# The second half of a macaron block's last feed-forward layer: 16 of its 22 row tiles by Strassen's scheme

## The reference, cut to what matters

```
h = rmsnorm(x, ffn2_pre_norm)
gate, up = split(h @ w_ffn2_in, 2)          # w_ffn2_in: 1024 x 5632
a = silu(gate) * up                         # a: 512 tokens x 2816
y = a @ w_ffn2_out                          # w_ffn2_out: 2816 x 1024
x = x + 0.5 * rmsnorm(y, ffn2_post_norm)
```

## Time and profile before

| | us |
|---|---|
| three runs, lowest, median, highest | 1472.89, 1472.93, 1472.98 |
| the profiled execution, first to last instruction (span) | 1471.1 |
| TensorE matmul busy | 1463.6 |
| VectorE, ScalarE busy | 735.7, 592.3 |
| the layer's second half, first to last matmul | 119.7 |

### The profile page before, as it was taken

One profiled execution on the slowest core, in us unless ns is written; L12 is line 12 of the kernel. 1 busy time (PEld: TensorE's weight loads), 2 busy tenths in 40 slices (PEclk: granted clock), 3 DMA queues, 4 the chain that ended last, 5 costly groups with the idle time before them and its releaser, 6 DMA issues.

```text
span 1471.1 us, 20399 instructions
## 1 busy us (share of the span) xinstructions
PE 1463.6 (99%) x7600; PEld 1226.3 (83%) x7600; DVE 735.7 (50%) x1219; ACT 592.3 (40%) x969; POOL 20.2 (1%) x35
## 2 busy tenths in 40 slices
PE   9999999999999999999999999999999999999998
PEld 7888888888898888888888888888889888888886
DVE  6444444224763455554257776654447544444223
ACT  5233223223543455554254654553345432323222
POOL 0000000000100000000000000000000000000000
PEclk9999999999999999999999999999999999999999
DMA  5322322334232222212322222223331323332332
GB/s 194 99 89 97 100 100 86 100 101 130 76 124 99 78 72 90 73 64 94 99 87 72 72 73 69 71 72 129 105 111 44 101 87 99 100 99 89 98 100 100
DMA packets 39399, 137.70 MB, mean 94 GB/s; under 512 B 4743, under 2 KB 4743, under 8 KB 39344
## 3 DMA queue, kind: packets, MB, share of 16 engines
q1 hardware_dynamic: 37728, 132.14, 27.9%
q0 software_dynamic: 1472, 4.76, 1.2%
q10 hardware_dynamic: 144, 0.04, 0.0%
HBM read 134.00 MB, written 2.13 MB: 93 GB/s over the span
## 4 chain that ended last, share of the span: by engine, by line
PE 99%; DMA 0%; DVE 0%; ACT 0%; issue 0%; DVEq 0%; SPq 0%; ACTq 0%
PE ps L333 28%; PE ps L335 27%; PE ps L334 27%; PE ps L1468 1%; PE ps L1204 1%; PE ps L1205 1%; PE ps L1206 1%; PE ps L1347 1%; PE ps L1346 1%; PE ps L1348 1%; PE ps L1828 1%; PE ps L1448 1%; PE ps L1848 1%; PE ps L1433 1%; PE ps L1815 1%; PE ps L1435 1%
## 5 line engine op out<-in xcount | busy, mean ns | idle before, releaser
L333 PE MATMUL ps<-hh,whi 128*128 128x512 f32 x1232 | 485.9, 394 | 0.0
L291 ACT ACTIVATE whi<-raw 128x1024 fp32r<-128x1024 f32 x232 | 245.7, 1059 | 585.4 <-PE ps L335 530.2
L334 PE MATMUL ps<-hl,whi 128*128 128x512 f32 x1232 | 480.0, 390 | 0.0
L335 PE MATMUL ps<-hh,wlo 128*128 128x512 f32 x1232 | 479.9, 390 | 0.0
L296 DVE TENSOR_TENSOR wlo<-raw,whi 128x1024 fp32r<-128x1024 f32 x232 | 284.1, 1225 | 368.1 <-ACT whi L291 368.0
L333 PEld LDWEIGHTS ps<-hh,whi 128*128 128x128 f32 x1232 | 231.4, 188 | 53.0 <-issue 2.8
L335 PEld LDWEIGHTS ps<-hh,wlo 128*128 128x128 f32 x1232 | 231.4, 188 | 48.9
L334 PEld LDWEIGHTS ps<-hl,whi 128*128 128x128 f32 x1232 | 231.6, 188 | 46.6 <-issue 0.2
L514 DVE TENSOR_TENSOR tmp<-ps,rstd 128x512 f32<-128x512 f32 x44 | 30.4, 690 | 118.8 <-PE ps L335 118.8
L333 PE MATMUL ps<-ah,whi 128*128 128x512 f32 (+1 forms) x192 | 71.6, 373 | 0.4 <-DVE wlo L296 0.4
L334 PE MATMUL ps<-al,whi 128*128 128x512 f32 (+1 forms) x192 | 71.3, 371 | 0.0
(11 more groups left out here) (318 smaller groups left out, 1854.1 us busy)
## 6 DMA issues: line engine op xcount, KB each, us to landing
raw<-in_wstream SPq DMA_DIRECT2D x238, 512.0 KB, 3.4
xt<-in_x_t SPq DMA_DIRECT2D x8, 256.0 KB, 5.3
out<-out_tok SPq DMA_DIRECT2D x8, 256.0 KB, 2.0
bias<-vec_dram POOLq DMA_DIRECT2D x8, 192.0 KB, 3.2
raw<-in_wstream SPq DMA_DIRECT2D x4, 256.0 KB, 4.4
bias<-vec_dram POOLq DMA_DIRECT2D x8, 128.0 KB, 3.4
raw_y<-in_wstream SPq DMA_DIRECT2D x2, 512.0 KB, 4.2
raw_x<-in_wstream SPq DMA_DIRECT2D x2, 512.0 KB, 4.1
```

What stands on the lines that cost most here:

```text
L291: nc.scalar.activation(whi[:, s, :], raw[:, s, :], ACT.Copy).then_inc(head_done, 1)
L333: nc.tensor.matmul(out, w, m, start=start, stop=False)
L334: nc.tensor.matmul(out, w, ml, start=False, stop=False)
L335: return nc.tensor.matmul(out, wl, m, start=False, stop=stop)
```

## The change

The last 16 row tiles of the second half are computed by a scheme of Strassen's kind (Winograd's form: 7 products, 4 sums of each operand, 7 joins). Tokens, columns and row tiles are each cut in two halves, so that both operands have four quarters. The even of the 16 tiles are one half, the odd the other; `kp` numbers the eight pairs, and a chunk `c` is two of them. In place of 8 products of quarters there are 7; each is 2 token tiles x 2 tiles x 3 = 12 matmuls a chunk (`quadrant`), with a block of its own that is one quarter of the weights of that chunk.

- The layer's first half is written out from turn 6 on for ACT and DVE (`pair`). The tile of `a` is kept whole (`a_raw`, in the place of `al`). Per pair, DVE makes four sums of 128 x 256 (`pair_sums`), each waiting for the one before; ACT makes the high parts of both tiles (1024 columns) and of three sums (768), and DVE the low parts (`pair_head`, `pair_low`). Pairs 6 and 7 get theirs in the second half.
- The second half has 34 blocks m for 22: 12 DIRECT ones (three quarters of each chunk, as they are), 16 SUMMED ones (four quarters of each chunk, which are loaded again and on which DVE first makes a sum in place, `w_sum`), and 6 plain ones of 24 matmuls for the first 6 row tiles.
- Split blocks have three buffers for two, and loaded ones a ring of six for two (`out_load`).
- Results of products are copied from PSUM by ACT (`leave`) and joined by DVE with what others hold (the joins).
- The new buffers lie where `x` by token and the gain row were. So POOL stores `x` to memory at turn 5 and loads it and the gain row again when the plain blocks begin.
- Some semaphores elsewhere are merged, with the same order of work.

The core of the diff (left out: the places of buffers, `t_sums`, `raw_slot`, `plain`, the definitions of most joins, which each are one DVE instruction of 128 x 512, and the merged semaphores):

```diff
+N_KP = 8
+N_PLAIN = FT - 2 * N_KP
+N_CHUNK = N_KP // 2
+AHEAD_KP = 6
+LAST = 2 * FIRST["ffn3_out"]
+DIRECT, SUMMED = 3 * N_CHUNK, 4 * N_CHUNK
+PLAIN_0 = DIRECT + SUMMED
+OUT_BLOCKS = PLAIN_0 + N_PLAIN
+RING = 6
...
+        a_raw = place("a_raw", [P, FT, S])
...
+        def pair_sums(dve, m):
+            k1, k2 = N_PLAIN + 2 * m, N_PLAIN + 2 * m + 1
+            raw_t = t_sums(m)[2].rearrange("p (t n) -> p t n", t=3)
+            a = [[a_raw[:, k, cols] for cols in TOKENS] for k in (k1, k2)]
+            if m < 2:
+                dve.wait_ge(sem("x_turned"), KT)
+            elif m < AHEAD_KP:
+                dve.wait_ge(sem("pool_stored"), 16 * (1 + TT))
+            else:
+                dve.wait_ge(block_done, LAST)
+            dve.wait_ge(sem("glu"), BEFORE[3] + k2 + 2)
+            nc.vector.tensor_tensor(raw_t[:, 1, :], a[1][1], a[0][1], ALU.subtract).then_inc(sem("t_sum"), 1)
+            dve.wait_ge(sem("t_sum"), 4 * m + 1)
+            nc.vector.tensor_tensor(a[0][1], a[0][0], a[0][1], ALU.subtract).then_inc(sem("t_sum"), 1)
+            dve.wait_ge(sem("t_sum"), 4 * m + 2)
+            nc.vector.scalar_tensor_tensor(out=raw_t[:, 0, :], in0=a[0][1], scalar=-1.0, in1=a[1][1], op0=ALU.mult,
+                                           op1=ALU.subtract).then_inc(sem("t_sum"), 1)
+            dve.wait_ge(sem("t_sum"), 4 * m + 3)
+            nc.vector.scalar_tensor_tensor(out=raw_t[:, 2, :], in0=raw_t[:, 0, :], scalar=-1.0, in1=a[1][0],
+                                           op0=ALU.mult, op1=ALU.subtract).then_inc(sem("t_sum"), 1)
+        def pair_head(act, m):
+            k1 = N_PLAIN + 2 * m
+            high, _, summed = t_sums(m)
+            flat = "p k n -> p (k n)"
+            act.wait_ge(sem("t_sum"), 4 * m + 2)
+            act.wait_ge(sem("glu"), BEFORE[3] + k1 + 3)
+            nc.scalar.activation(ah[:, k1:k1 + 2, :].rearrange(flat), a_raw[:, k1:k1 + 2, :].rearrange(flat),
+                                 ACT.Copy).then_inc(sem("a_head"), 1)
+            act.wait_ge(sem("t_sum"), 4 * m + 4)
+            nc.scalar.activation(high, summed, ACT.Copy).then_inc(sem("a_head"), 1)
+        def pair_low(dve, m, part):
+            k1 = N_PLAIN + 2 * m
+            flat = "p k n -> p (k n)"
+            dve.wait_ge(sem("t_sum"), 4 * m + 4)
+            dve.wait_ge(sem("a_head"), BEFORE[3] + k1 + part + 1)
+            high, low, whole = t_sums(m) if part else [x[:, k1:k1 + 2, :].rearrange(flat) for x in (ah, al, a_raw)]
+            nc.vector.tensor_tensor(low, whole, high.bitcast(F32), ALU.subtract
+                                    ).then_inc(sem("a_tail"), 1)
...
+            def pair(m):
+                j = N_PLAIN + 2 * m
+                for k in (j, j + 1):
+                    turn(k, False)
+                if m < AHEAD_KP:
+                    pair_head(act, m)
...
+            def glu_whole(j):
+                dve.wait_ge(sem("silu"), BEFORE[n] + j + 2)
+                dve.wait_ge(sem("up"), BEFORE[n] + j + 1)
+                nc.vector.tensor_tensor(a_raw[:, j, :], silu[:], tmp[:, 1, :], ALU.mult
+                                        ).then_inc(sem("glu"), 1)
+            def pair(m):
+                j = N_PLAIN + 2 * m
+                gated(j, 0)
+                tail(dve, first + j, 0)
+                if 0 < m <= AHEAD_KP:
+                    for part in range(2):
+                        pair_low(dve, m - 1, part)
+                up(j, 1)
+                tail(dve, first + j, 1)
+                glu_whole(j)
+                gated(j + 1, 0)
+                tail(dve, first + j + 1, 0)
+                up(j + 1, 1)
+                tail(dve, first + j + 1, 1)
+                glu_whole(j + 1)
+                if m < AHEAD_KP:
+                    pair_sums(dve, m)
...
+        BANK_U, BANK_V, BANK_W, BANK_Z = (4, 5), (6, 7), (2, 3), (0, 1)
+        ROW_BANK = (BANK_U + BANK_V, BANK_W + BANK_Z)
+        FIRST_HALF = (2, 3, 0, 1)
...
+        def split_of(m):
+            s = m % 3
+            return (whi[:, s, :], wlo[:, s, :]) if s < 2 else (whi_2[:], wlo_2[:])
+        def out_source(m):
+            if m < DIRECT:
+                return (m % 3) * N_CHUNK + m // 3 if m % 3 < 2 else 3 * N_CHUNK + m // 3
+            if m < PLAIN_0:
+                c, q = divmod(m - DIRECT, 4)
+                return (3, 2, 0, 1)[q] * N_CHUNK + c
+            return SUMMED + m - PLAIN_0
+        def out_load(sp, m):
+            if m < 4:
+                sp.wait_ge(split_done, LAST + m - 1)
+            elif m < 2 + RING:
+                sp.wait_ge(block_done, LAST)
+            else:
+                sp.wait_ge(split_done, LAST + m - RING + 1)
+            sp.dma_start(raw_of(m), wstream[LAST + out_source(m)]).then_inc(raw_landed(m)[0], 16)
+        def out_head(act, m):
+            if m >= DIRECT and m < PLAIN_0:
+                act.wait_ge(sem("s_sum"), m - DIRECT + 1)
+            else:
+                act.wait_ge(*raw_landed(m))
+            act.wait_ge(block_done, LAST + max(0, m - 2))
+            nc.scalar.activation(split_of(m)[0], raw_of(m), ACT.Copy).then_inc(head_done, 1)
+        def out_tail(dve, m):
+            dve.wait_ge(head_done, LAST + m + 1)
+            if DIRECT <= m < PLAIN_0:
+                dve.wait_ge(sem("s_sum"), 4 * ((m - DIRECT) // 4 + 1) if (m - DIRECT) % 4 else m - DIRECT + 3)
+            high, low = split_of(m)
+            nc.vector.tensor_tensor(low, raw_of(m), high.bitcast(F32), ALU.subtract).then_inc(split_done, 1)
+        def w_sum(dve, m):
+            c, q = divmod(m - DIRECT, 4)
+            w22, w21, w11, w12 = (DIRECT + 4 * c + i for i in range(4))
+            a, b = ((w22, w21), (w21, w11), (w11, w22), (w12, w11))[q]
+            for x in {0: (w22, w21), 1: (w11,), 2: (), 3: (w12,)}[q]:
+                dve.wait_ge(*raw_landed(x))
+            if q:
+                dve.wait_ge(sem("s_sum"), m - DIRECT)
+            nc.vector.tensor_tensor(raw_of(a), raw_of(a), raw_of(b), ALU.add).then_inc(sem("s_sum"), 1)
...
+            def quadrant(m, c, x, banks, start):
+                pe.wait_ge(split_done, LAST + m + 1)
+                pe.wait_ge(sem("a_tail"), BEFORE[3] + N_PLAIN + 1 + 2 * (2 * c + 2))
+                for i in range(2):
+                    for k in range(2):
+                        high, low = tile_of(x, 2 * c + k)
+                        last = onto(ps[:, banks[i], :], high[:, at_token[i]], low[:, at_token[i]], m, k,
+                                    start and c == 0 and k == 0, c == N_CHUNK - 1 and k == 1)
+                last.then_inc(block_done, 1)
...
+            for c in range(N_CHUNK):
+                quadrant(3 * c, c, "b11", BANK_U, True)
+                quadrant(3 * c + 1, c, "b21", BANK_V, True)
+                quadrant(3 * c + 2, c, "t4", BANK_W, True)
+            for c in range(N_CHUNK):
+                m = DIRECT + 4 * c
+                quadrant(m, c, "t1", BANK_Z, True)
+                pe.wait_ge(sem("q_left"), 4)
+                quadrant(m + 1, c, "t3", BANK_W, True)
+                quadrant(m + 2, c, "t2", BANK_U, False)
+                pe.wait_ge(sem("q_joined"), 2)
+                quadrant(m + 3, c, "b22", BANK_V, True)
...
+                    for t in order:
+                        if b == 0 and half == 0 and t < 2:
+                            pe.wait_ge(sem("q_left"), 7 + t)
+                        if b == 0 and half == 1:
+                            pe.wait_ge(sem("q_joined"), 9 + t if t < 2 else 5 + t - 2)
+                        for k in range(2):
+                            last = plain(m, half, t, k)
...
+            for m in range(2, OUT_BLOCKS - 1):
+                out_head(act, m)
+                if m == 4:
+                    pair_head(act, AHEAD_KP)
+                if m == 7:
+                    pair_head(act, AHEAD_KP + 1)
+                if m == DIRECT - 1:
+                    act.wait_ge(block_done, LAST + DIRECT - 2)
+                    for i in range(2):
+                        leave(i, p1, BANK_U)
+                if m == DIRECT + 1:
+                    act.wait_ge(block_done, LAST + DIRECT)
+                    for i in range(2):
+                        leave(i, q4, BANK_W)
+                if m == PLAIN_0:
+                    act.wait_ge(block_done, LAST + PLAIN_0 - 1)
+                    for i in range(2):
+                        leave(i, u2, BANK_U)
+                    for i in range(2):
+                        act.wait_ge(sem("q_left"), 5 + i)
+                        act.wait_ge(sem("q_joined"), 1 + i)
+                        nc.scalar.activation(ps[:, BANK_U[i], :], c11_part[i], ACT.Copy).then_inc(sem("q_left"), 1)
+            for n in range(TT - 1):
+                square(0, n)
+            out_head(act, OUT_BLOCKS - 1)
+            square(0, TT - 1)
...
+            def join(into, bank, other):
+                nc.vector.tensor_tensor(into, ps[:, bank, :], other, ALU.add).then_inc(sem("q_joined"), 1)
```

(122 more changed lines are left out.)

192 lines of the change are left out of this document (119 added, 73 removed).

## The result

| | before | after |
|---|---|---|
| runs of the comparison, median (lowest to highest), us | 1472.91 (1472.43 to 1472.98) | 1462.64 (1462.35 to 1463.12) |
| profiled execution, span, us | 1471.1 | 1460.6 |
| second half, first to last matmul start, us | 119.49 | 109.03 |
| matmuls | 7600 | 7552 |

The ratio is 0.9931, 95% interval 0.9917 to 0.9945: 10.3 us faster. The forecast was 1462.5.

The account below looks back on a forecast made before the run. The prediction took PE, streaming matmuls without a gap at full clock, as the bound. Removing 48 matmuls (-10.9 us) plus block 3's 0.45 gave -10.4: span 1460.7, median 1462.5 us, range 1461.8 to 1466.5.

Parts of the forecast that it names:

- What is removed: Second half: 336 matmuls in place of 384, so 48 fewer at 0.2267 us each, a gain of 10.9 us.
- First half at nothing: Turns 6 to 21: added sums and low parts cost nothing, with 2.9 us of cover before PE wants the split.
- Block 3: Second half: its load waits for block 1's split, so 0.34 us late plus 0.1 slow restart; 0.45 taken.
- Summed blocks: Second half: four sums and four low parts per chunk take DVE 9.4 us against PE's 10.88, 86% full.
- The ring: Second half's loaded-weight buffers: loop of landing plus 6.3 us, 9.7 at landing 3.4, under 10.88 per chunk; limit is landing 4.6.
- The burst: Loads queued at the second half's start: four land at 7.5, 8.9, 10.4, 11.8 us; the sign said landings up to 5.
- `x` again: POOL's five reloads, issued at the first plain block, land 10 to 12 us later; DVE asks at 13.3.
- The sum: Whole span: -10.9 + 0.45 = -10.4, so 1471.1 becomes 1460.7; median 1.83 above, 1462.5 us.
- B: Rival: DVE's chain becomes the bound in the second half, 1464.5 to 1468, about 1466 us; chance 0.08.
- C: Rival: late weights in the second half, one us per chunk per us of landing beyond 4.6; up to 1482; chance 0.04.
- D: Rival: `x` reloaded late around the plain blocks; six us of slack, then each us costs one; 1467; chance 0.02.
- E: Rival: the change doesn't do what it says and saves no products, time 1473 us; chance 0.01.

Follow-up runs that it names:

- experiment 1: Changed kernel with the first summed product of each chunk computed twice, putting the 48 saved matmuls back: 1473.61 us, ratio 1.0005 to the kernel before.

## Why the prediction was right

- **What is removed.** 10.9 us for 48 matmuls: confirmed by the half and by computing them again (10.97).
- **First half at nothing.** No wait of PE in it, 174.18 us from turn 6 on as before, and 2.6 us of cover, measured; 2.6 was in the working.
- **Block 1, margin 0.15.** Split at 1347.99 and PE on time at 1348.13. **Block 2**, split foretold at T0 + 4.9: 4.95. **Block 6**, 16.3: 16.2. **Block 15**, 40.5: 40.4.
- **Block 3, 0.34 and 0.1.** 0.27 and 0.11 in the timeline, 0.41 when it is taken away. The load took 3.5 us where 3.4 was taken. In the eight other profiles in which this part is as in the changed kernel, the distance there was 0.47 to 0.78 for the 0.50 here, in the same order as the landing times of this load, 3.45 to 3.74.
- **Summed blocks.** I said 86% of DVE, then "near 90%"; it was 81% in the window. Starts with work ready are 1.13 to 1.15 us apart, and the length of 1.22 overlaps the next. Sums in place took 1.22, joins 0.68 to 0.70, copies into PSUM 0.60 to 0.61, as taken from rows of the same size.
- **The ring.** The weakest step, without harm. I put landings at 3.4 for the steady stretch; they were 3.7 in the median and up to 4.9, which is over the 4.6 that I had named as the sign of being wrong. The loop foretold at 9.7 was 9.7 for block 21 and 10.9 for block 25: there no slack was left, and the DVE wait of 0.35 shows it. PE did not notice. That DMA was "half full" said nothing about how long one load takes among others.
- **The burst.** "Up to 5" did not fit my own working: it had the four loads landing at T0 + 7.5 to 11.8, and the last of them is issued at T0 + 4.4, which makes 7.4 us. They landed at T0 + 7.5, 9.4, 10.7 and 11.9, up to 7.5 after their issue. The working came true, the sign drawn from it did not.
- **`x` again.** The loads landed before DVE asked, and the gain was scaled at 1435.41, without a wait.
- **The sum.** Span 1460.7 foretold, 1460.6 measured. A tenth of agreement is partly luck: T0 0.46 early and the tail 0.35 long nearly cancel, and I had foreseen neither.
- **The rivals.** B begins at about one microsecond more per chunk, C at a split's delay of the loads, D at some 8.6 us of delay. None had begun. E is excluded by the count of 7552 and by experiment 1. The prices of B, C and D all left out the slow matmuls that follow a long wait. The rule that would make D likelier is that a POOL load's descriptors wait for a DVE operation that uses both its ports, such as a float32 copy (the Trainium skill, "SBUF — State Buffer", "SBUF: two separate sides"). For these loads no run here tests it: the DVE operations beside POOL's five issues had two inputs each, and the issues took 0.53 us each.

## What to carry to other kernels

Where PE streams without a gap, matmuls left out are worth their spacing, and the question is only whether the other queues still come in time. That can be worked out block by block from the timeline before: who issues, who lands, who splits, in the order written. Take the landing time from loads that are queued as densely as the new ones will be, not from the sparse stretch before. Look at the one load that closes the loop, not at a median over all. Price a wait of PE of over 2 us with the slow matmuls that may follow it: an expectation without them can still come out, by luck.

## What the runs showed of the hardware

- **Waits and the clock.** Waits of up to 1.3 us left PE at 2.4 GHz. One of 2.2 us (in two kernels) was followed by nine slow distances of matmul starts, 3.7 us in place of 2.0, at a granted clock of 0.54 and 0.53, near the 1.2 GHz level, so that it cost almost double. Length alone doesn't decide: with the loads two splits late, one of 2.65 us kept the full clock, the next, of 4.03, was followed by 0.50, and a later one of 2.33 by slow matmuls again. What decides is not settled here.
- **Loads under load.** The same 512 KB took 3.4 us in the median before, at a DMA share of 0.28, and 3.7 (3.2 to 4.9) in blocks 12 to 27 of the changed kernel, where the share was 0.60 in the window from 1378 to 1421. Two of these sixteen were issued after the one before had landed (blocks 17 and 19); they took 3.3 and 3.2. Of four issued in 2.1 us the last took 7.5, and the one behind them 8.0.
